# The context's products of a second block, done in the expert stages of the first

## What is computed

```python
def _layer(x, ctx, c, c_ctx, w_ada, b_ada, norm_g, w_in, ..., update_ctx):
    ...
    hx = _rmsnorm(x, norm_g) * (1.0 + scale_x) + shift_x
    hc = _rmsnorm(ctx, norm_g) * (1.0 + scale_c) + shift_c

    px = hx @ w_in
    a_k, a_v, b_k, b_v, a_q, b_q, a_z, b_z, g_a, g_b = _split(px, SPLIT_SIZES)
    pc = hc @ (w_in if update_ctx else w_in[:, :KV_COLS])
```

## Time and profile before

| | us |
|---|---|
| median of 3 runs | 3613.65 |
| the runs | 3609.46, 3613.65, 3622.63 |
| span of the profiled execution | 3606.1 |
| expert stage 0, first pass to last down | 637.7 to 1131.2 |
| expert stage 1 | 1565.4 to 2062.7 |
| second block, layer 0: row norm, qkv, pairs, ga | from 2096.2, 2118.5, 2326, 2600 |

### The profile page before, as it was taken

The page is one execution under the profiler, slowest core; times in us unless marked ns, Lnnn a source line. Parts: engine busy times, 40 slices in busy tenths (PEclk is TensorE's granted clock), DMA queues, the critical chain, the costliest instruction groups (busy, mean ns, idle before and its releaser), DMA issues. The chain is left out here.

```text
span 3606.1 us, 39767 instructions
## 1 busy us (share of the span) xinstructions
PE 3162.4 (88%) x16263; PEld 1614.8 (45%) x16263; DVE 986.4 (27%) x1980; ACT 770.1 (21%) x1592; POOL 241.5 (7%) x228
## 2 busy tenths in 40 slices
PE   8998997887684998787786669999999989999999
PEld 4447963322221446332222235565544435556444
DVE  2426634100003007330000030275500220176202
ACT  1412250100001006110000043245400012245200
POOL 0015410000000000100000011100000001100000
PEclk9999998988897999898898889999999999999999
DMA  6431424999997432389999731201011121121121
GB/s 206 170 128 59 205 95 187 379 428 424 427 428 296 150 143 46 105 338 427 428 426 427 303 118 35 69 23 48 24 47 47 59 47 41 45 46 48 47 83 46
DMA packets 168840, 639.59 MB, mean 177 GB/s; under 512 B 63476, under 2 KB 65906, under 8 KB 142672
## 3 DMA queue, kind: packets, MB, share of 16 engines
q1 hardware_dynamic: 143664, 463.02, 34.1%
q10 hardware_dynamic: 16416, 144.71, 9.5%
q0 software_dynamic: 8576, 29.26, 2.3%
HBM read 584.38 MB, written 56.50 MB: 178 GB/s over the span
## 5 line engine op out<-in xcount | busy, mean ns | idle before, releaser
L1550 PE MATMUL banks<-weight_ring,experts_xT 128*32 128x512 f32 (+1 forms) x2240 | 372.0, 619 | 50.3 <-DMA weight_ring<-in_moe_w 30.9
L2549 PE MATMUL banks<-weight_ring,cols 128*128 128x512 f32 x672 | 296.8, 604 | 14.2 <-PEq L2688 8.2
L1568 PE MATMUL banks<-weight_ring,experts_hT 128*32 128x512 f32 (+1 forms) x1216 | 242.3, 633 | 72.6 <-DMA weight_ring<-in_moe_w 70.7
L1550 PEld LDWEIGHTS banks<-weight_ring,experts_xT 128*32 128x32 f32 (+1 forms) x2240 | 109.7, 122 | 259.1 <-issue 251.9
L2549 PEld LDWEIGHTS banks<-weight_ring,cols 128*128 128x128 f32 x672 | 129.6, 194 | 179.9 <-issue 179.9
L2549 PE MATMUL banks<-weight_ring 128*128 128x512 f32 x480 | 207.0, 593 | 3.7 <-PEq L2527 1.9
L1568 PE MATMUL banks<-cols,experts_hT 128*32 128x512 f32 (+1 forms) x448 | 168.2, 647 | 24.7 <-DMA cols<-in_moe_w 24.7
L3057 PE MATMUL banks<-cols,weight_ring 128*128 128x512 f32 x416 | 182.9, 592 | 1.9 <-PEq L283 1.9
L1550 PE MATMUL banks<-cols,experts_xT 128*32 128x512 f32 (+1 forms) x640 | 174.3, 602 | 2.3 <-DMA experts_slot<-in_moe_w 2.1
L663 PE MATMUL banks<-cols,weight_ring 128*128 128x512 f32 x384 | 171.0, 601 | 1.0 <-PEq L283 1.0
L1550 PE MATMUL banks<-experts_slot,experts_xT 128*32 128x512 f32 (+1 forms) x448 | 163.2, 621 | 7.2 <-issue 7.2
(11 more groups left out here) (441 smaller groups left out, 4414.0 us busy)
## 6 DMA issues: line engine op xcount, KB each, us to landing
weight_ring<-in_moe_w SPq DMA_DIRECT2D x96, 2048.0 KB, 21.6
weight_ring<-in_moe_w ACTq DMA_DIRECT2D x36, 2048.0 KB, 22.7
cols<-in_moe_w SPq DMA_DIRECT2D x22, 2048.0 KB, 21.9
experts_slot<-in_moe_w SPq DMA_DIRECT2D x20, 2048.0 KB, 23.5
cols<-in_moe_w ACTq DMA_DIRECT2D x18, 2048.0 KB, 20.3
weight_ring<-in_w_in SPq DMA_DIRECT2D x16, 2048.0 KB, 7.9
weight_ring<-in_w_ada SPq DMA_DIRECT2D x12, 2048.0 KB, 11.2
weight_ring<-in_a_w_in SPq DMA_DIRECT2D x8, 2048.0 KB, 11.7
```

Of the source, the lines that this page charges most:

```text
L1550: mm = pe.matmul(bank[a:a + n, :], self.xT[:, 4 * part + k, a:a + n], slots(r, part)[:, k, c:c + 512], start=part == k == 0, stop=part == ...
L1568: mm = pe.matmul(self.out[c][a:a + n, :], self.hT[:, f, a:a + n], slots(r, 2)[:, f, c * 512:c * 512 + 512], start=f == 0, stop=f == 3)
L2549: mm = pe.matmul(ps[i % 8][0:u.shape[0], 0:u.shape[1]], u.lhs(w, k), u.rhs(w, k), start=k == 0, stop=k == u.kd - 1)
```

## The change

The context's normed columns `CT` are made in `stage_layer_norm` of ln_mix0 (`context=CT`): the rows are loaded ahead of `gb`, ScalarE squares and scales them, TensorE turns them behind `keep_busy`, ScalarE scales and shifts into `CT` (1 MB), which is kept in DRAM between the layers. The products `hc @ w_in` are cut into eleven groups of at most 512 columns (`CTX_GROUPS`), each of two units that fill one bank (kb with vb one unit). A group's weights, 1024 rows of 2 KB (kb: 1 KB), become one more load in the order of the expert stage, through the same nine slots; unit 0 stands ahead of the second half of its pass, unit 1 behind the down of the pass before. In layer 0 there are six groups in passes 3, 5, 7, 9, 11 and 13 and two (zb, ga1) behind the last down; in layer 1 one (kb) in pass 8 and two (gb0, gb1) behind. ScalarE empties unit 0, VectorE unit 1, and GpSimd's queue stores them to DRAM. The second block loads them back where it had computed them and leaves out its context products; the norms of the context's keys and queries stay there, and the sigmoid of the context's gates becomes one ScalarE operation in each gate stage. The weights of `w_in` for x are loaded in the second block as before. Besides, `gb` of an expert stage is loaded after the last down, a few parameters of the second block's norms earlier, and the constants are reordered so that the buffers of the stores lie over those that only DeltaNet uses.

```diff
+CTX_GROUPS = context_groups()
+CTX_IN_PASS = [{3: "ka", 5: "qa", 7: "qb", 9: "va", 11: "za", 13: "ga0"}, {8: "kb"}]
+CTX_BEHIND = [["zb", "ga1"], ["gb0", "gb1"]]
+BEHIND_SLOT = 3
...
-def weight_uses():
+def weight_uses(l):
     out = []
     for p in range(NP + 1):
         if p < NP:
-            out += [(r, part, ("first_half", "up")[part], p) for part in range(2) for _, _, r in reversed(PASSES[p].tiles)]
+            out += [((r, 0), "first_half", p) for _, _, r in reversed(PASSES[p].tiles)]
+            if p in CTX_IN_PASS[l]:
+                out.append((CTX_IN_PASS[l][p], "context", CTX_IN_PASS[l][p]))
+            out += [((r, 1), "up", p) for _, _, r in reversed(PASSES[p].tiles)]
         if p:
-            out += [(r, 2, "down", p - 1) for _, _, r in reversed(PASSES[p - 1].tiles)]
+            out += [((r, 2), "down", p - 1) for _, _, r in reversed(PASSES[p - 1].tiles)]
     return out
...
+    def product(self, pe, n, w):
+        if n and (n not in self.behind or n == self.behind[0]):
+            pe.wait_ge(*self.emptied(n - 1))
+        for x, at in self.pieces(n):
+            dst = self.bank(n)[:, at:at + x[-1]]
+            for k in range(KD):
+                if x[0] == "cols":
+                    mm = pe.matmul(dst, w[:, k, x[2]:x[2] + P], self.CT[:, k, :], start=k == 0, stop=k == KD - 1)
+                else:
+                    mm = pe.matmul(dst, self.CT[:, k, x[2] * P:(x[2] + 1) * P], w[:, k, x[3]:x[3] + x[-1]], start=k == 0,
+                                   stop=k == KD - 1)
+        mm.then_inc(*self.filled.up(n))
+
+    def empty(self, eng, n):
+        eng.wait_ge(*self.filled.at(n))
+        if n >= 2:
+            eng.wait_ge(*self.stored_at[n - 2])
+        if n in self.by_act:
+            eng.activation(self.buf[:, n % 2, :], self.bank(n), ACT.Copy).then_inc(*self.act_emptied.up(n))
+        else:
+            eng.tensor_copy(self.buf[:, n % 2, :], self.bank(n)).then_inc(*self.dve_emptied.up(n))
...
-        behind_down = {m: LAST_USE[m - MOE_SLOTS][1] for m in range(MOE_SLOTS, 3 * NE) if LAST_USE[m - MOE_SLOTS][0] == "down"}
+        earlier = {m: max(x for x in here if x < m and x % MOE_SLOTS == m % MOE_SLOTS) for m in here if m >= MOE_SLOTS}
+        behind_down = {m: last_use[x][1] for m, x in earlier.items() if last_use[x][0] == "down"}
 
         def load_weights(eng, m, expert):
-            r, part = LOADS[m]
+            if loads[m] in CTX_GROUPS:
+                g = CTX_GROUPS[loads[m]]
+                eng.wait_ge(*released(earlier[m]))
+                eng.dma_start(context_slot(g.name), A["w_in_2"][0].rearrange("(k p) n -> p k n", p=P)[:, :, g.c0:g.c0 + g.width]
+                              ).then_inc(own[m % MOE_SLOTS], 16)
+                return
+            r, part = loads[m]
...
                     elif p + 1 < NP:
                         B.turn(pe, p + 1)
+                    if p in CTX_IN_PASS[l]:
+                        context_product(CTX_IN_PASS[l][p], 0)
                     weights_landed(tiles, 1, "up", p)
                     B.gate_up(pe, tiles, 1, slots)
...
                         B.down(pe, p - 1, PASSES[p - 1].tiles, slots)
+                    if p in CTX_IN_PASS[l]:
+                        context_product(CTX_IN_PASS[l][p], 1)
...
+                for name in CTX_BEHIND[l]:
+                    for i in range(2):
+                        context_product(name, i)
                 pe.wait_ge(*V.at(f"m{NT - 1}"))
                 keep_busy(K, pe, 0, 3)
...
+                    if p in CTX_IN_PASS[l]:
+                        C.empty(act, C.of(CTX_IN_PASS[l][p])[0])
                     B.gated(act, p)
...
+                behind = [n for n in C.behind if n in C.by_act]
+                C.empty(act, behind[0])
...
+                    for n in behind[1 + t:2 + t]:
+                        C.empty(act, n)
...
-    tiles = [(K.H, Xn, t) for t in range(NT)] + [(B.C, Cn, t) for t in range(2)]
+    tiles = [(K.H, Xn, t) for t in range(NT)] + [(B.C, Cn, t) for t in range(2) if l]
...
+                if off and with_ctx:
+                    units.append(None)
+                else:
+                    units.extend(cols_units(i, KD, width, xT, [(0, n)], [c], plain, cols_to(dst, off), ("act",)))
...
-            units = both_rows(0, KD, 512, K.HT, B.CT, 0, 512, sig(0), with_ctx, ("act",))
-            units += both_rows(1, KD, 512, K.HT, B.CT, 0, 512, sig(512), with_ctx, ("act",))
-            stage_products(K, f"gate{i}_{l}", 2, units)
+            units = both_rows(0, KD, 512, K.HT, B.CT, 0, 512, sig(0), False, ("act",))
+            units += both_rows(1, KD, 512, K.HT, B.CT, 0, 512, sig(512), False, ("act",))
+            stage_products(K, f"gate{i}_{l}", 2, units, context=(M[:, NT:, :], ("ga", "gb")[i]) if with_ctx else None)
```

More of the change, by code:

```diff
@@ L1677, in landed @@
             i = m % MOE_SLOTS
-            earlier = l * sum(n >= RING for n in range(i, 3 * NE, MOE_SLOTS))
-            return own[i], 16 * (earlier + m // MOE_SLOTS + (i >= RING))
+            return own[i], landed_before[i] + 16 * len([x for x in here if RING <= x <= m and x % MOE_SLOTS == i])
         chosen = [f"{x}{p}" for p in range(SELECTED) for x in ("picked", "selected", "based")]
@@ L1904, in _ @@
                                                 K.H[:, t, :], None).then_inc(X.scattered, 16)
+                for n in range(len(C.units)):
+                    if n not in C.behind:
+                        C.store(pool, n)
                 pool.wait_ge(*S.at("stored"))
@@ L2131, in _ @@
                 centre(t)
+                for n in behind[1:]:
+                    C.empty(dve, n)
                 dve.wait_ge(*S.at("rs"))
@@ L2513, in cols_units, with stage_products @@
     return out
-def stage_products(K, name, ngroups, units, ahead=None, stores=()):
+def stage_products(K, name, ngroups, units, ahead=None, stores=(), context=None):
     ps = K.ps
@@ L3048, in _ @@
                 for m in range(last):
-                    if m < M:
+                    if m < M and units[m] is not None:
                         u = units[m]
```

325 lines of the change are left out of this document (254 added, 71 removed).

## The result

| | before | after |
|---|---|---|
| median | 3613.65 | 3625.70 |
| runs | 15, 3607.76 to 3622.63 | 15, 3619.86 to 3630.07 |
| span of the profiled execution | 3606.1 | 3621.2 |

The ratio is 1.0029, with a 95% interval of 1.0021 to 1.0036: slower by 12 us, inside the range (3540 to 3635) and inside the 0.5% that counts as the same, but on the other side of 3613.65 than the forecast of 3593, and just above the 3570 to 3625 of the forecast's own case A. The spans of the two profiled executions differ by 15.1 us.

A forecast was written before the change was run, and what follows sets the result against it. Weights through DMA were taken to bound the expert stages, TensorE the second block. Removed 146.2 us, added 19.7 outside the expert passes, 84 in stage 0 and 22 in stage 1: 3613.65 - 20.5 = 3593 us, range 3540 to 3635.

The forecast's parts named there:

- case A: Whole kernel: most of the gain is given back in the expert stages by slots and packet turns, 3570 to 3625; chance 0.58.
- qkv: Second block's qkv stage: 13 context units of 256 columns, vb and va are removed from TensorE's path, 62.2 us less.
- stage 1: Layer 1's expert stage: one group, kb, lands late and adds its stores and bytes, 22 us more.
- packet turns between the queues: Expert stages: queues share by packets, not bytes, so a group beside a full SP queue takes 45 us instead of 5.6.
- The steady period: Expert stage 0, four-expert passes: two passes, one with a group, take 78.8 us against 63.9 by bytes before.
- Stage 0: Layer 0's expert stage: six groups through the nine slots add 84 us, taken between 95 and 74.
- the forecast's full 55: Expert stage 0, four-expert passes: four periods cost 14.9 us more each, less 4 for the first, 55 in all.
- the half taken between the two clocks: Expert stage 0: 95 us more, or 74 if the clock never falls in 12 products; 84 taken.
- the pairs: Second block's attention pairs: 64 z fills of 256 columns at 0.43 us each are removed, all counted, 27.7 us less.
- the tails: Behind each layer's last down: units and late loads add 4.1 us in layer 0, 7 in layer 1; 11 taken.
- case D: Second block: pairs or gates give back their gain, through ScalarE-bound steps or late context loads; 3600 to 3640, chance 0.04.
- B (bytes alone): Expert stages: loads share fairly and groups land in time; stage 0 grows 43 to 51 us; 3540 in all, chance 0.24.
- C's mechanism: Expert stages: groups on ScalarE's queue hold up next rows and first-half weights, four-expert passes too; likelier 3635 to 3650, chance 0.14.

## Why the prediction was wrong, step by step

**Right.** qkv (62.2), the gates (50.9 against 50.5), the row norm (6.3 against 5.8) and stage 1 (24.2 against 22). The mechanism named for the pair passes, packet turns between the queues, is in the trace in its numbers, and one edit bears it out (long rows land sooner). The steady period was right in size.

**Right in sum, partly by luck.** Stage 0 took 88.1 us more against 84, but the 84 were 40 for the pair passes and 44 for the four-expert ones, where 26.5 and 59.1 were measured (with 2.5 behind them). The two misses nearly cancel. For the four-expert passes the forecast's full 55 was nearer than the half taken between the two clocks.

**The steps that failed.** The sign came out wrong by two steps of about the same weight, the pairs (15.8 us) and the tails (15.1); with only one of them the sum would still have been a gain of some 5 us.

*The pairs.* "They go wholly only if the attention's own chain has room below 5.9 us a step; ... so I count all of it." The average big step did come out at 5.9 (5.47 and 6.33 in turn), but only half of the gain was there: the small pairs take 3.34 us instead of 2.92, because their one fill of 512 columns leaves a wait of 0.55 for the exp, and the waits at the start of a head's four pairs, which had a fill before them, lie open (steps of 7.4 and 7.5). TensorE's gaps of over 0.15 us from the first score to the next stage were 10.3 us before and 24.3 after, 14.0 of the missing 15.8. Putting the same products back cost 13.4 us. This was in case D, at 0.04 and with no price of its own; it should have been a term of the sum with two ends, 27.7 and about 12. (By its own rows the 27.7 is 27.1: a third of 7.18 less 5.91, 64 times.)

*The tails.* 11 forecast, 26.2 measured; both grew by over 10, which the forecast had named as the sign that its reading of the combine was wrong. I had ScalarE's copy of the third unit in the sum, but with the units starting at the down; they start 5.1 us later behind layer 0 and 7.2 behind layer 1, and the first two run slow. Moving the copy gave back 4.4 and 4.6 us. The move of `gb` behind the down, which I costed at nothing, sets layer 0's result rows back by 5 us (behind layer 1 they come 8 us later, mostly beside gb1's weights), but loading it behind the store gave, by itself, 0 and 1.2 us. With both edits the tails' floor is TensorE's sequence at 34.9 us, 6.4 and 6.9 more than `keep_busy` before.

**Right in size for a partly wrong reason.** In the four-expert period TensorE waited 2.4 us for the group and not 9.6 (SP's queue was nearly empty, and the group landed after 9.6 us where the forecast had 18.0, whose own terms add up to 17.6), and ahead of the second half and the down 3.2 and 9.6 instead of 0 and 7.6. The runs point at the round of slots: 13 loads and not 12 go through nine slots in two passes, so that more of them are asked for only when the half just ahead has freed their slot. Bytes gone or units gone left the waits for expert weights ahead of the second half and the down, and the DMA engines not full (shares of 0.89 and 0.94 over such passes); taking the group out of the round took away all but one of them, that for a down, which was there before, and 44 us with them. But that edit also moved the weights to another queue with fewer packets, asked for them a pass ahead and spread the units, so how the 44 us divide isn't shown. The load cut to an eighth, with a group that lands in 3.8 us and a period of 76 to 78 still, speaks for the round of slots; a run with both bytes and units gone, and the slots kept, would have shown it.

**The rivals.** B (bytes alone) gave the wrong time for this change, but its price, 43 us for stage 0, is what the same work costs once it has a place of its own: 44.0. The sign named for it (groups that land in under 10 us) was no test: in three four-expert passes they did, and the period was 76 to 79 all the same. C's mechanism, rows stuck behind a group, is in pass 3 (21.5 us) and pass 5 (6.3 us); in the four-expert passes it isn't. The Trainium skill, "DMA: Bandwidth & Descriptors", section "Queues, rings and completion order", weighed in the forecast, says that an engine drains a whole packet, typically 9 to 17 descriptors, from one queue before it changes. This case's trace does not agree: 2 KB rows beside 16 KB rows start 0.70 us apart, one row of each. The equal counts, on which the forecast went, don't show it by themselves, since bundles of equal length in both queues would give them too.

## What to carry to other kernels

Work that fits into an engine's idle time can still be dear if its data goes through the buffers whose turnaround causes that idle time: give a guest its own small buffer and ask for its data early, and it costs its bytes (here 7 us per group instead of 15). Small rows beside a queue of large ones take the time of the large ones (35 to 48 us for 2 MB here, against 9 to 10 beside a nearly empty queue), so issue them where the other queue is empty or a whole pass ahead, and not behind large loads of their own queue. And where fills hide a chain, only part of a removed fill comes back: here 12 us for context fills that the forecast had at 27, and 20.5 for the next 40. Price it by the chain's own step. A total that comes out right may hold two misses: compare the parts too.

## What the runs showed of the hardware

Two and three DMA queues shared the engines by equal numbers of packets (454 to 458; 282 to 284 to 251) whatever the packets' size, also with one of them on GpSimd's queue, and two hardware queues changed at each row (2 KB rows 0.70 us apart beside rows of 16 KB). Rows of 1 KB from DRAM were packets of 4 KB on GpSimd's queue. The broadcast load of the norm's parameters, 128 times the same 4 KB row from DRAM, took more of the engines for its bytes than the store beside it: from 1230.9 to 1239 us, 54.1% for 1.05 MB against 16.9% for 0.52, or 0.27 us a row against 0.17. The store landed 5 us late beside it, and 2.9 us after issue without it.
